# 96 instead of 64 prompt tokens outside the dense expert passes of a two-layer step, on one core

## What is computed

```
def block(xb):                                       # n tokens of width 1024
    q = (xb @ w_q).reshape(n, 8, 2, 128)
    s = einsum('thcd,hckd->thck', q, keys)           # 8 heads, 2 halves, 128 keys each
    s_top, i_top = top_k(s, 16)
    cand = s_top[:, :, 0, :, None] + s_top[:, :, 1, None, :]
    best, pos = top_k(cand.reshape(n, 8, 256), 16)   # 8 * 16 = 128 experts for a token
    experts = ...                                    # key 0 * 128 + key 1
    gate = softmax(best)
    act = gelu(einsum('thkd,td->thk', u_tab[experts], xb))
    return einsum('thk,thkd->td', gate * act, v_tab[experts])
```

## Time and profile before

| | us |
|---|---|
| runs of the kernel, median (lowest to highest) | 4166.35 (4151.7 to 4177.22) |
| the profiled execution, its own time | 4161.64 |
| its span, first to last instruction | 4159.7 |
| hidden stage of layer 0, from the first matmul of unit 0 to the output stage | 765.1 to 1522.1 |
| output stage of layer 0 | 1522.1 to 2150.2 |
| hidden stage of layer 1 | 2742.0 to 3502.4 |
| output stage of layer 1 | 3502.4 to 4141.2 |

### The profile page before, as it was taken

How to read it: one execution, slowest core, us unless ns; L and a number is a source line. 1 busy time by engine, 2 the same in 40 slices (tenths; PEclk the granted TensorE clock), 3 DMA queues, 4 the chain that set the end, 5 groups by cost and what they waited for, 6 DMA issues and landing times. The chain is left out here.

```text
span 4159.7 us, 67721 instructions
## 1 busy us (share of the span) xinstructions
PE 3938.3 (95%) x26750; PEld 3599.2 (87%) x26750; DVE 2854.7 (69%) x4937; ACT 1649.8 (40%) x3060; POOL 1505.8 (36%) x871
## 2 busy tenths in 40 slices
PE   8996989999999999999989888999999999999998
PEld 7983878899889989999979867889988998999997
DVE  6456556999555448888863486699955553888886
ACT  4222223366555523333332353336655552333332
POOL 0000003345554445555530000334555544555552
PEclk9997999999999999999999989999999999999999
DMA  7612045388998878788832423538899887777783
GB/s 214 186 48 89 4 120 108 86 227 225 297 271 232 225 255 283 276 291 281 269 115 84 120 72 81 110 84 226 226 295 268 235 227 246 282 272 284 275 281 126
DMA packets 607036, 820.87 MB, mean 197 GB/s; under 512 B 76161, under 2 KB 540666, under 8 KB 586242
## 3 DMA queue, kind: packets, MB, share of 16 engines
q1 hardware_dynamic: 562260, 664.73, 54.0%
q0 software_dynamic: 41472, 151.01, 11.0%
q10 hardware_dynamic: 2990, 0.82, 0.1%
HBM read 683.65 MB, written 128.33 MB: 195 GB/s over the span
## 5 line engine op out<-in xcount | busy, mean ns | idle before, releaser
L3074 PE MATMUL ps<-h_parts,u_parts 128*128 128x448 f32 x6144 | 1307.4, 369 | 30.2 <-POOL u_parts L2422 12.4
L3074 PEld LDWEIGHTS ps<-h_parts,u_parts 128*128 128x128 f32 x6144 | 1139.9, 189 | 124.6 <-POOL u_parts L2422 24.4
L2422 POOL TENSOR_TENSOR u_parts<-u_turned,u_parts 128x1024 fp32r<-128x1024 f32 x256 | 619.3, 2420 | 718.7 <-ACT u_parts L2417 717.3
L3503 PE MATMUL ps<-w_parts,v_parts 128*128 128x448 f32 x4080 | 852.0, 367 | 3.3 <-POOL w_parts L3295 3.3
L3503 PEld LDWEIGHTS ps<-w_parts,v_parts 128*128 128x128 f32 x4080 | 765.0, 188 | 72.3 <-issue 4.0
L2409 DVE STREAM_TRANSPOSE u_turned<-u_rows 128x1024 f32<-128x1024 f32 x256 | 317.8, 1241 | 445.1 <-POOL u_parts L2422 234.4
L3503 PE MATMUL ps<-first_w,first_v 128*128 128x448 f32 x2064 | 439.5, 369 | 7.4 <-PEq L2975 7.4
L3503 PEld LDWEIGHTS ps<-first_w,first_v 128*128 128x128 f32 x2064 | 390.1, 189 | 43.3 <-issue 8.1
L2417 ACT CAST u_parts<-u_turned 128x1024 fp32r<-128x1024 f32 x256 | 269.2, 1051 | 231.2 <-DVE u_turned L2409 226.7
L2958 ACT ACTIVATE hidden<-ps 128x448 f32<-128x448 f32 x256 | 137.9, 539 | 403.1 <-PE ps L3074 273.1
L2964 ACT ACTIVATE onehots<-onehots,choice 128x128 f32<-128x128 f32 x896 | 285.6, 394 | 9.6 <-DVE onehots L2938 5.3
(11 more groups left out here) (677 smaller groups left out, 5841.3 us busy)
## 6 DMA issues: line engine op xcount, KB each, us to landing
u_rows<-in_peer_u_dram SPq DMA_DIRECT2D x1024, 128.0 KB
u_rows<-in_peer_v_dram SPq DMA_DIRECT2D x86, 1024.0 KB, 6.5
hidden_tiles<-hidden SPq DMA_DIRECT2D x256, 224.0 KB
gate_matrices<-h SPq DMA_DIRECT2D x56, 1024.0 KB
gates<-gate_matrices SPq DMA_DIRECT2D x32, 1792.0 KB, 8.9
u_turned<-hidden_tiles SPq DMA_DIRECT2D x256, 224.0 KB
v_rows<-in_peer_v_dram SPq DMA_DIRECT2D x42, 1024.0 KB
arena<-in_ada_w_dram SPq DMA_DIRECT2D x32, 1024.0 KB, 6.6
```

The source lines that it names most:

```text
L2422: s.nc.gpsimd.tensor_tensor(q.uTs[:, (n + 1) % 3, 1], q.uT[:, n % 2], q.uTs[:, (n + 1) % 3, 0].bitcast(F32), ALU.subtract).then_inc(q.u_re ...
L3074: ins = mm(ps[:, n % 2, 0:TD], q.uTs[:, (n + 1) % 3, wp, k, :], q.hs[:, xp, k, 0:TD], start=k == 0 and (wp, xp) == (0, 0), stop=k == DT - ...
L3503: ins = nc.tensor.matmul(ps[:, o, 0:TD], q.vs[n % 3][:, vp, o * P:(o + 1) * P], q.ws[n % 3][:, wp, 0:TD], start=n == 0 and (vp, wp) == (0, ...
```

## The change

96 prompt tokens leave the dense passes, in two sets (`SETS`). The first set has 64 tokens with two slots a transfer, as before. The second has 32 tokens, which lie on the partitions four times, with four slots a transfer, so 32 more transfers serve it. The dense passes keep 416 columns, and there are 104 quads instead of 112.

- `GATHER_STEPS` becomes 96: 96 dots at `DOT_RATE` 1.0 a unit, and 96 `add_row` at 1.26 units apart.
- The small set's token rows wait in a third plane of `q.hot` that no one else uses. After dot 63 ScalarE copies them into the PSUM tile that held the large set's rows (8 copies of 32x512), and dot 64 comes at least four units later.
- The output stage keeps two sums and turns them with 16 matmuls instead of 8.

By the loop's own counting the dots are in units 13 to 76 and 80 to 110 (before: 14 to 116), the last prompt tile is routed in unit 47 (before: 40), the samples' picks are made in unit 54 (before: 46), and their 8 dots are in units 60 to 74 (before: 52 to 66).

```
-GATHERED = 64
-TD = T - GATHERED
-SLOT_SIDES = P // GATHERED
-GATHER_STEPS = NH * TOPK // SLOT_SIDES
+LARGE, SMALL = 64, 32
+TD = T - LARGE - SMALL
+SETS = ((LARGE, P - LARGE, 0), (SMALL, P - LARGE - SMALL, LARGE))
+GATHER_STEPS = LARGE + SMALL
...
-DOT_RATE = 0.62
+DOT_RATE = 1.0
...
     def row_dot(dve, j):
         if j == 0:
-            dve.wait_ge(q.t_copied.sem, q.t_copied.at(2))
+            dve.wait_ge(q.t_copied.sem, q.t_copied.at(3))
+        if j == LARGE:
+            dve.wait_ge(q.t_copied.sem, q.t_copied.at(7))
...
-                    while dots_due >= 1.0 and dots < GATHER_STEPS:
+                    while dots_due >= 1.0 and dots < GATHER_STEPS and (dots != LARGE or n >= row_unit[LARGE - 1] + 4):
...
+                if row_unit[LARGE - 1] == n:
+                    act.wait_ge(q.t_dotted.sem, q.t_dotted.at(LARGE))
+                    for side in range(P // SMALL):
+                        part = slice(side * SMALL, (side + 1) * SMALL)
+                        for i in range(2):
+                            ins = nc.scalar.copy(token_rows[part, i * 512:(i + 1) * 512], small_rows[i])
+                        ins.then_inc(q.t_copied.sem, 1)
...
-ROW_FIRST, ROW_STEP = 3, 185
+ROW_FIRST, ROW_STEP = 3, 126
...
                         if o == 0:
-                            pe.wait_ge(q.t_summed.sem, q.t_summed.at(GATHER_STEPS + 1))
-                        ins = nc.tensor.matmul(ps[:, o, TD:T], q.row_sum[:, o * P:(o + 1) * P], q.both_sides, start=True, stop=True)
+                            pe.wait_ge(q.t_summed.sem, q.t_summed.at(GATHER_STEPS + 2))
+                        nc.tensor.matmul(ps[:, o, TD:TD + SMALL], q.row_sums[:, 1, o * P:(o + 1) * P], q.four_sides,
+                                         start=True, stop=True)
+                        ins = nc.tensor.matmul(ps[:, o, TD + SMALL:T], q.row_sums[:, 0, o * P:(o + 1) * P], q.two_sides,
+                                               start=True, stop=True)
```

More of the change, by code:

```diff
@@ L2749, in peer_hidden @@
     token_rows = ps[:, 4:6, :].rearrange("p b c -> p (b c)")
+    small_rows = [f32(q.hot[0:SMALL, i, 2]).rearrange("p t w -> p (t w)") for i in range(2)]
     s_scores = r.scores[:].rearrange("p (c k) -> p c k", c=2)
@@ L2903, in routing @@
             if t == 0:
-                own = slice(P - GATHERED, P)
                 dve.wait_ge(q.picks.sem, q.picks.at(1))
-                link(v.tensor_scalar(r.rowf[own], q.picked[own, 0, :], float(NK), float(layer * NK * NK), ALU.mult, ALU.add))
-                for side in range(SLOT_SIDES):
-                    to, of = slice(side * GATHERED, (side + 1) * GATHERED), slice(side * GATHER_STEPS, (side + 1) * GATHER_STEPS)
-                    v.tensor_copy(r.tgate[to], q.picked[own, 2, of])
-                    ins = v.tensor_tensor(r.rows[to], r.rowf[own, of], q.picked[own, 1, of], ALU.add)
+                link(v.tensor_scalar(r.rowf, q.picked[:, 0, :], float(NK), float(layer * NK * NK), ALU.mult, ALU.add))
+                for count, first, step in SETS:
+                    own = slice(first, first + count)
+                    for side in range(P // count):
+                        to, of = slice(side * count, (side + 1) * count), slice(side * count, (side + 1) * count)
+                        v.tensor_copy(r.tgate[to, step:step + count], q.picked[own, 2, of])
+                        ins = v.tensor_tensor(r.rows[to, step:step + count], r.rowf[own, of], q.picked[own, 1, of], ALU.add)
                 ins.then_inc(q.t_picked.sem, 1)
@@ L3064, in _ @@
                     for k in range(DT):
-                        ins = nc.tensor.transpose(ps[0:GATHERED, 2 + k // 4, (k % 4) * P:(k % 4 + 1) * P],
-                                                  s.h[:, k, TD:T], s.ident[:])
+                        for i, (first, last) in enumerate(((TD + SMALL, T), (TD, TD + SMALL))):
+                            ins = nc.tensor.transpose(
+                                ps[0:last - first, 2 + 2 * i + k // 4, (k % 4) * P:(k % 4 + 1) * P],
+                                s.h[:, k, first:last], s.ident[:])
                     ins.then_inc(q.t_turned.sem, 1)
@@ L3514, in peer_outputs @@
     q.out_sum.close(NK - 1 + DT)
-    q.t_summed.close(GATHER_STEPS + 1)
+    q.t_summed.close(GATHER_STEPS + 2)
     for i in range(V_PLACES):
```

35 lines of the change are left out of this document (22 added, 13 removed).

## The result

The changed kernel took 4037.2 us in the median of 4 runs (4031.2 to 4050.7), the kernel before 4159.0 us in the median of 4 beside it (4147.3 to 4177.2). The ratio is 0.9711, with a 95% interval of 0.9676 to 0.9746: faster by 2.9%. The forecast was 4049, with 4008 to 4094. The profiled execution of the changed kernel took 4031.2 us, the shortest of the four.

What follows compares the result with a forecast made beforehand. PE bounds the output stages and the hidden stage's second half, DVE the routing, DMA the samples' gathers. A layer gains 4.6 + 11 + 43 = 58.6 us, two 117; 4161.6 - 117 = 4044.4, plus 4.7 to the median: 4049, range 4008 to 4094.

Steps and rivals of the forecast that it cites:

- Part 1: Dense matmuls, 32 fewer columns: each gets 14.2 ns shorter, 43.6 us a stage where PE is always the bound.
- Part 2: Output stage: DVE keeps up at 529 to 560 us of work, PE loses nothing, gain 43 us a layer.
- Part 3: Hidden stage up to unit 52: DVE bounds while tokens are routed; 7.6 us less 3 for late gathers, gain 4.6 us.
- the 3 us for late gathers: Hidden stage up to unit 52: a few gathers land after their dots need them and stop DVE, from 0 to 15 us.
- Part 4: Hidden stage from unit 52: PE gains 30 us, transfers cost 17 and two small terms 2, gain 11 us.
- The loss of 17 and 2 us: Hidden stage from unit 52: 17 us to DMA transfers, 2 us to eight ScalarE copies and eight more PE transposes.
- the gelu waiting longer than 49.6 us: Hidden stage: expected sign that the gelu waits for its store longer than the 49.6 us of the kernel before.
- My 23.9 MB for before: Hidden stage, units 55 to 72 of the kernel before: bytes counted without the samples' 8.4 MB, 32.3 MB in all.
- The DMA is no limit: Rival: hidden stage loses only where DVE is the bound, gains 36 us a layer; 159 us in all, 4007; chance 0.13.
- the hidden stage gives nothing: Rival: late gathers and store waits leave only the output stage's 43 us a layer, 4080 us; chance 0.19.
- matmuls don't get shorter: Rival: something other than columns sets 203 ns a matmul, so only the quads go; about 4190 or 4166 us; chance 0.04.
- DVE sets the pace: Rival: in the output stage DVE keeps its waits and the stage gets 40 to 71 us longer, 4214 to 4276; chance 0.04.

Runs made afterwards that it cites:

- the widths: Two runs with narrower output-stage matmuls: changed kernel at 384 and 400 columns, 173 and 180 ns a matmul; kernel before at 432 and 440, 196 and 200 ns.
- the packed updates: Changed kernel with one gathered state update in each output-stage unit from unit 3 until all 96 are done, instead of 126 in 100 units: 4036.6 us.

## Why the prediction was right, point by point

- **Part 1, 14.2 ns a matmul.** In the hidden stages a unit with a quad went from 5.76 us to between 5.37 and 5.42, which is 14 to 16 ns a matmul. The output stages show 16.0 and 20.0: 202.7 and 206.7 became 186.7. This is the term that was mis-sized: I priced columns from a projection, while the two stages before had periods of their own. The formula that I took from the Trainium skill (TensorE: Matmul & The Clock Gate, Back-to-back issue gap) is given there for an isolated matmul and not for a stream with a weight load for each, so it was no measure of this term. Ten kernels with 416 columns give 20 output stages; 9 lasted 579 to 581 us and 11 lasted 584 to 586, the same code in both groups (periods of 186.7 and of 188.3). With 448 there are 628.1 us once and 638.8 to 641.6 three times. The profile of before had one of each, that of after two of the lower, and that is luck of the two profiles. What picks the period is open; no run was made for it.
- **Part 2, 43 us a layer.** 47.8 and 59.4: 3072 x 16.0 and 20.0 ns are 49 and 61 us, less 1 to 2 at the ends of the stages, where 8 closing matmuls more stand. That DVE keeps up is shown by the widths and by the packed updates. My 529 to 560 us for it was too high, 515.6 were measured. The 32 updates cost 36.3 and 31.2 us against the run without them (479.3 and 483.7), near my 39. But all else became 20 us cheaper, not 10: 10 in `gate_rows`, as I had it, and 9 in the 63 `add_row` that were there before (128.3 to 119.4 us). The transfers came out at 306 GB/s and a share of 0.87, for 304 and 0.88.
- **Part 3, 4.6 us.** 4.7 and 5.2. The step, DVE as the bound while tokens are routed, is shown: taking bytes away does nothing there, taking routing out of the units gives 14.2 us. It is the allowance that sets the length of a unit there, and not the amount of DVE work as a whole. Without the 32 tokens DVE has 18.5 us less to do from the turn of unit 2 to that of unit 52, and the stretch is only 2.2 us shorter (287.0 against 289.2). The size of my 4.6 us was partly luck. From the turn of unit 2 to that of unit 52 it took 289.2 us where my count gave 285.6, and the 3 us for late gathers were no such thing: gathers are not among the waits there. DVE worked 285.5 us of it, 3.6 more than the 242.0 + 39.9 of my count.
- **Part 4, 11 us.** 7.7 and 12.0 (449.5 to 441.8, and 452.2 to 440.2). The loss of 17 and 2 us against PE's gain was 18.2 in the run without the 32 tokens. It lies where I put it, and the mechanism is two things: the bytes of the gathers among the samples' rows (halved, 17 and 13 us of units 52 to 80 come back), and the two places of the gelu, whose store waits for SP's issue of u rows and then lands late (a third place: 4 and 6 us there, 8 and 7 in the stage, partly the same ones). Which of the two delays of the store matters was not tried: no run issues it ahead of the loads or from another engine. The eight copies on ScalarE were not tried by themselves either; in layer 0 they took 4.49 us, and PE waited 1.34 us for the one-hots behind them. My sign "the gelu waiting longer than 49.6 us" was a poor one: in the 120 us of the earlier trace rows it waits 35.8 us now, and it is the longest single wait that grew. My 23.9 MB for before should be 24.3 (11 gathers in those units), which changes nothing.
- **Rivals.** "The DMA is no limit" and "the hidden stage gives nothing" are refuted by the table of the pieces, "matmuls don't get shorter" and "DVE sets the pace" by the timelines.
- **The sum.** 117 predicted, 131.0 in the span and 121.8 between the medians; the profiled execution of before lay 2.6 us over its median, that of after 6.1 under its own. In the spans the output stages gave 21 us more than my 86, the hidden stages 1.6 less than my 31.2, the rest 5.8 less than my nothing. So part of the fit is luck: the largest term was a fifth too small, and the rest made up for some of it. Of the 12 us between 4049 and 4037.2, 7 are the base, since I started from a median of 4166.35 and it was 4159.0 in the four runs, and 5 the gain.

## What to carry to other kernels

A planner's allowance that was tuned for one length of the dense unit is a part of every change to that length: where the trace shows one engine at 98% in a stretch, give the allowance a run of its own, on the kernel before too, so that one knows what belongs to the change. A DMA share over 1 is no bound by itself; ask which short-lived buffer is waiting for its store, what is issued ahead of that store, and whether taking bytes away moves that stretch. Price a matmul from the period in its own stage, and count on it taking more than one value.

## What the runs showed of the hardware

**The period of a matmul is not a function of its columns alone.** Float32 matmuls of 128x416 with their weight loads settled at 186.7 or at 188.3 ns for a whole stage, and those of 128x448 at 202.7 or 206.7, at a granted clock of 0.99 or 1.00 over the stage. In the run without the 32 tokens the two layers of one execution have one each. The Trainium skill (TensorE: Matmul & The Clock Gate, Wait — 56ns, not 53.3ns?) gives columns over 2.4 GHz and about 2.5 ns for back-to-back matmuls; for these matmuls no run agrees, since the piece on top is 13 to 20 ns and grows with the columns.

**A stall of PE costs more than its length.** Two windows of the changed kernel behind the wait of 8.15 us:

```profile
1118.40:1124.50 6.10, 6.09 (x25) 5.94 (x26) 4.16 (x5) 5.46 (x13) 4.56 (x3) 0.74 1.10 252
1124.50:1129.85 5.35, 5.35 (x33) 5.35 (x32) 2.42 (x5) 3.11 (x7) 4.88 (x4) 1.00 1.11 371
```

The granted clock was 0.74 in the first, a mean of its levels of 1.2 and 2.4 GHz, and full again in the next; the 24 matmuls took 1.5 us more than the next 24. The prediction had no term for that. The second window moved 371 GB/s, so the 323 that I took for the pace of crowded transfers is no ceiling; the 384 columns above kept 329 GB/s up for 540 us.
